# Gated delta scan of a hybrid encoder layer: decaying and adding the state on VectorE instead of GpSimd and VectorE

## The reference

```python
def step(S, xs):
    u0c, wc, qkc, qgc, kdc, glc = xs
    u = u0c - jnp.einsum('bhck,bhkv->bhcv', wc, S)
    o = jnp.einsum('bhck,bhkv->bhcv', qgc, S) + jnp.einsum('bhij,bhjv->bhiv', qkc, u)
    S = glc[..., None, None] * S + jnp.einsum('bhck,bhcv->bhkv', kdc, u)
    return S, o

S, o = lax.scan(step, S0.astype(jnp.float32), (u0, wk, qk, qg, kd, gl))
```

## Time and profile before

| | |
|---|---|
| timed executions, median (lowest to highest) | 2307.71 us (2307.32 to 2307.99) |
| profiled execution, its own time | 2306.37 us |
| its span, first to last instruction | 2305.1 us |
| mean granted TensorE clock, share of full speed | 0.92 |
| `delta_net`, about | 457 to 695 us of the span |
| busy: PE, DVE, ACT, POOL | 2001.3, 1026.7, 686.0, 534.5 us |

### The profile page before, as it was taken

How to read it: one execution, slowest core, us unless ns; L and a number is a source line. 1 busy time by engine, 2 the same in 40 slices (tenths; PEclk the granted TensorE clock), 3 DMA queues, 4 the chain that set the end, 5 groups by cost and what they waited for, 6 DMA issues and landing times. The chain is left out here.

```text
span 2305.1 us, 28427 instructions
## 1 busy us (share of the span) xinstructions
PE 2001.3 (87%) x10881; PEld 1829.8 (79%) x10881; DVE 1026.7 (45%) x1317; ACT 686.0 (30%) x1266; POOL 534.5 (23%) x465
## 2 busy tenths in 40 slices
PE   3999999455883779669999798999999999999997
PEld 3999998254772668559988676899999999999996
DVE  4222443475333321151134122566667575756666
ACT  4112222435552322331131031422222223232322
POOL 2000000232221141430021051223233232332320
PEclk9999999677785779779999899999999999999998
DMA  3222120210003030321013310111010111111012
GB/s 111 59 77 69 56 57 13 72 28 19 28 28 121 1 128 1 127 92 46 10 73 110 126 57 28 46 28 55 27 55 27 55 37 45 48 34 55 27 37 89
DMA packets 122324, 127.00 MB, mean 55 GB/s; under 512 B 10261, under 2 KB 104574, under 8 KB 121950
## 3 DMA queue, kind: packets, MB, share of 16 engines
q1 hardware_dynamic: 117630, 120.89, 16.7%
q10 hardware_dynamic: 3714, 4.76, 0.7%
q0 software_dynamic: 896, 0.19, 0.0%
HBM read 109.86 MB, written 15.96 MB: 55 GB/s over the span
## 5 line engine op out<-in xcount | busy, mean ns | idle before, releaser
L2579 PE MATMUL ffn_banks<-h_hi,up_hi 128*128 128x384 f32 x1056 | 352.9, 334 | 1.8 <-PEq L116 1.8
L2579 PE MATMUL ffn_banks<-h_hi,up_lo 128*128 128x384 f32 x1056 | 353.0, 334 | 0.0
L2579 PE MATMUL ffn_banks<-h_lo,up_hi 128*128 128x384 f32 x1056 | 352.8, 334 | 0.0
L2754 DVE TENSOR_TENSOR h<-h,ffn_banks 128x512 f32<-128x512 f32 x396 | 270.0, 687 | 148.9 <-PE ffn_banks L2614 142.4
L2724 DVE SCALAR_TENSOR_TENSOR ffn_conv_out<-ffn_conv_in,vec,ffn_conv_out 128x1168 f32<-128x1168 f32 x88 | 206.7, 2349 | 128.3 <-ACT ffn_conv_out L2645 122.5
L548 PE MATMUL proj_banks<-x_hi,in_w_hi 128*128 128x384 f32 (+1 forms) x648 | 218.7, 338 | 0.0
L548 PE MATMUL proj_banks<-x_hi,in_w_lo 128*128 128x384 f32 (+1 forms) x648 | 217.3, 335 | 0.0
L548 PE MATMUL proj_banks<-x_lo,in_w_hi 128*128 128x384 f32 (+1 forms) x648 | 217.3, 335 | 0.0
L2579 PEld LDWEIGHTS ffn_banks<-h_hi,up_hi 128*128 128x128 f32 x1056 | 198.2, 188 | 3.0 <-issue 2.0
L2579 PEld LDWEIGHTS ffn_banks<-h_lo,up_hi 128*128 128x128 f32 x1056 | 198.2, 188 | 0.9
L2579 PEld LDWEIGHTS ffn_banks<-h_hi,up_lo 128*128 128x128 f32 x1056 | 198.2, 188 | 0.0
(11 more groups left out here) (409 smaller groups left out, 3612.3 us busy)
## 6 DMA issues: line engine op xcount, KB each, us to landing
up_raw<-in_w_up SPq DMA_DIRECT2D x44, 512.0 KB, 5.8
in_w_raw<-in_w_in SPq DMA_DIRECT2D x22, 512.0 KB, 4.1
down_raw<-in_w_down SPq DMA_DIRECT2D x22, 512.0 KB, 3.6
mem_k_one<-in_cache_mem_k SPq DMA_DIRECT2D x8, 1024.0 KB, 4.9
spill<-mixT SPq DMA_DIRECT2D x10, 576.0 KB, 5.3
wo_w_raw<-in_w_o SPq DMA_DIRECT2D x8, 512.0 KB, 3.7
h<-in_x_prompt SPq DMA_DIRECT2D x8, 512.0 KB, 7.6
mkv_w_raw<-in_w_mk SPq DMA_DIRECT2D x8, 512.0 KB, 3.8
```

The lines of the kernel that those rows point to most:

```text
L2579: ins = nc.tensor.matmul(banks[:, NP * s + p, 0:TC], wt[:, s, k, :], x[:, k, TC * p:TC * p + TC], start=(n == 0), stop=(n == 3 * KD - 1))
L2754: nc.vector.tensor_tensor(to, to, banks[:, d_bank[n % 5], :], ALU.add).then_inc(added, 1)
```

## The change

POOL's `decayed` and its buffer go. VectorE multiplies the old state by the decay and adds the product in one `scalar_tensor_tensor` for each head, in place.

```diff
-        S, Sg, u = (ph.sb(n, [P, HEADS, P]) for n in ("state", "state_decayed", "u"))
+        S, u = (ph.sb(n, [P, HEADS, P]) for n in ("state", "u"))
...
-            def decayed(e, c):
-                n = 2 * (e - 1) + c
-                if n:
-                    pool.wait_ge(s_done, n)
-                end = P * tile_of(e) + 64 * c + 63
-                nc.gpsimd.tensor_tensor(Sg[:], S[:], up[:, :, end:end + 1].to_broadcast([P, HEADS, P]), ALU.mult
-                                        ).then_inc(sg_done, 1)
-
...
             for e in range(1, E_ALL):
-                decayed(e, 0)
                 if e + 1 < E_ALL:
                     q_up(e + 1)
-                decayed(e, 1)
                 if e + 1 < E_ALL:
                     k_tail(e + 1)
                 if e == 1:
...
             def new_state(e, c):
                 n = 2 * (e - 1) + c
                 dve.wait_ge(s_product, n + 1)
-                dve.wait_ge(sg_done, n + 1)
-                nc.vector.tensor_tensor(S[:], Sg[:], banks[2][:], ALU.add).then_inc(s_done, 1)
+                if n:
+                    dve.wait_ge(s_done, n)
+                else:
+                    dve.wait_ge(cleared, 1)
+                    dve.wait_ge(up_done, 3)
+                end = P * tile_of(e) + 64 * c + 63
+                for h in range(HEADS):
+                    ins = nc.vector.scalar_tensor_tensor(S[:, h, :], S[:, h, :], up[:, h, end:end + 1], banks[2][:, h, :],
+                                                         ALU.mult, ALU.add)
+                ins.then_inc(s_done, 1)
```

More of the change, by code:

```diff
@@ L959, in delta_net @@
          l5_wide, rk_done, kd_done, qg_done, z_done, z_copied, x_done, xt_ready, solved, u0_copied, wt_copied,
-         one_ready, one_used, u_s_done, so_done, kds_done, ws_done, u_done, s_product, o_done, sg_done, s_done, o_copied,
+         one_ready, one_used, u_s_done, so_done, kds_done, ws_done, u_done, s_product, o_done, s_done, o_copied,
          squared, rooted, inverted, o_scaled, o_turned, gated, kdm_done, sample_product, sample_decayed,
@@ L966, in delta_net @@
              "z_copied", "x_done", "xt_ready", "solved", "u0_copied", "wt_copied", "one_ready", "one_used", "u_s_done",
-             "so_done", "kds_done", "ws_done", "u_done", "s_product", "o_done", "sg_done", "s_done", "o_copied",
+             "so_done", "kds_done", "ws_done", "u_done", "s_product", "o_done", "s_done", "o_copied",
              "squared", "rooted", "inverted", "o_scaled", "o_turned", "gated", "kdm_done", "sample_product",
```

## The result

The changed kernel took 2319.05 us (median of five, 2314.01 to 2320.37) against 2307.32 us before: ratio 1.0047, 95% interval 1.0033 to 1.0062. The forecast was 2312.8 us, range 2309.0 to 2317.0; the direction was right, the size was not. Timed again beside later experiments, the same kernel gave a ratio of 1.0034 (1.0022 to 1.0047). Its 11 executions average 2317.4 us, and all 108 executions of the kernel before, in all series of measurements, 2307.7. So the loss to be explained is 9.8 us (ahead of rounding), of which 5.1 were forecast. Single executions of one kernel scatter with a standard deviation of 1 to 3 us, in one kernel of 5, so I compare means of groups where I can and give the half-width of their 95% interval where it matters.

What follows compares the result with a forecast made beforehand. VectorE was taken to bound the elimination, TensorE and ScalarE holding each other up the scan. Elimination +4.8 and last tile +0.3 gave +5.1 us on 2307.7: 2312.8 us, range 2309.0 to 2317.0.

Steps and rivals of the forecast that it cites:

- POOL's moved work in the elimination: In delta_net's elimination, four POOL instructions move in and one goes, so it ends 4.8 us later; bounds 0 and 5.7.
- The rival that it is hidden: Moved POOL instructions do not delay VectorE in the elimination; total 2308.0 us, no change; chance 8%.
- not before 545: Sign in the new profile: ScalarE's widening at about 548.1; the forecast is wrong if it still starts before 545.
- The 5.75 us: Upper bound for the elimination's growth, if VectorE gets nothing done during POOL's instructions, as under the exclusive lock.
- Nothing comes back at the scan's start: At the scan's start sample_state(0)'s 2.98 us wait for POOL goes, but this gives no time back.
- Four instructions: In new_state, four take 1.15 us for 0.69, +0.46 a step; only the last tile pays, +0.3, bounds 0 and 0.7.
- the state loop: Rival in the scan: each of 16 steps pays its 0.46 in full, 7.4 us more, total 2320; chance 6%.
- The sum, 4.8 + 0.3: Whole kernel: elimination's 4.8 plus the last tile's 0.3 makes +5.1 us.
- the change should add the same to both: The profiled run and the timed median both grow by 5.1 us: 2306.37 to 2311.5 and 2307.7 to 2312.8.
- The clock rival: Scan meets the granted clock otherwise: 2311.1 or 2309.4, upward 2314.5; downward side 16%, upward counted with the forecast.
- point 3: The part on new_state's four instructions for one: +0.46 a step, +0.3 us on the path in the last tile.

Runs made afterwards that it cites:

- e2: Kernel before, with only POOL's k_tail(2), masked(2), qk_mask(2) and sample_decay(0) moved ahead of decayed(1, 1); 2314.59 us, ratio 1.0027.
- e1: Changed kernel with POOL again waiting for the scan's first new state, so the four POOL instructions leave the elimination; 2314.19 us, ratio 1.0023.
- e9: Changed kernel with the dropped semaphore sg_done still allocated, used by nothing, the buffer still dropped; 2313.76 us.
- e12: Changed kernel measured once more, unaltered, on the chip of e9; 2317.19 us.
- e13: Changed kernel with one other semaphore cleared twice at the stage's end, giving SyncE's list its old length; 2314.52 us.
- e5: Kernel before, with one idle VectorE product of 256 elements ahead of the addition of step 14's state; 2308.97 us, ratio 1.0007.
- e3: Kernel before, with 11 idle VectorE products of 256 elements behind the elimination as a plain delay; 2315.65 us, ratio 1.0031.
- e11: Changed kernel with POOL held ahead of k_tail(0) until the elimination's result is there, and semaphore sg_done kept, used by nothing; 2301.62 us, ratio 0.9970.
- e7: e1 with both the unused buffer state_decayed and the unused semaphore kept at their old places; 2306.97 us, ratio 0.9995.
- e15: e1 measured again, unaltered; 2316.31 us.

## Why the prediction was wrong in its size

1. *POOL's moved work in the elimination, +4.8:* right, 4.7 us (4.65 by VectorE's timeline, 4.76 by ScalarE's wait), and shown alone by e2 (+5.5 for four instructions without one removed) and undone by e1. The rival that it is hidden is out: the widening starts at 547.24, not before 545. The exclusive-lock rule of the Trainium skill ("SBUF — State Buffer", section "SBUF: two separate sides") names the mechanism, and the trace agrees that VectorE's instruction is held for nearly all of POOL's, 2.45 us beside 2.52. The 5.75 us that the prediction worked out by that rule was too high, as the rows had said.
2. *Nothing comes back at the scan's start:* right; sample_state(0) now waits 1.87 us for TensorE.
3. *Four instructions, +0.46 a step, on the path in the last tile alone, +0.3:* right on the instructions (+0.43) and on the place, too small in the price. The wait is 0.40 us, but the eight products behind it run at 1.2 GHz and take 0.9 us more, so that the profile's scan is 1.3 us longer, as it is in the profiles of e9 and e12 (149.5 and 149.6 us; e13's took 151.9). TensorE waits for the state in no middle tile, so the state loop is not the limit. That the wait brings the low clock is supported by e5, where a wait of 0.43 us put there alone is followed by the same slow products; by time e5 puts it at 1.0 to 1.6 us, with an interval that reaches down to none.
4. *The sum, 4.8 + 0.3, and that "the change should add the same to both":* this step failed, in two ways. First, a term was missing. The change drops a semaphore, its diff says so, and I costed the wait and not the clearing. It makes SyncE's list one instruction shorter, which moves a pause onto a load that is waited for: 3.1 us here, 4.5 with POOL quiet. Second, a delay does not cost itself. The idle 5.0 us of e3 cost 7.6 by means (2315.5 against 2307.9 of its chip), e2's 5.5 cost 6.7, and with the list's length restored the changed kernel loses 6.7 for its 5.1. The clock rival had the mechanism and only counted its upward side with the forecast. In e3's profile it is in the scan itself, as the windows of its scan show beside the kernel before's 148.25 us at 0.78:

```profile
548.27:702.13 153.86, 128.01 (x752) 116.02 (x752) 46.59 (x90) 86.25 (x252) 42.94 (x38) 0.75 0.10 28
```

The same 752 matmuls, moved by 5.0 us, took 5.6 us longer at a clock of 0.75 in this execution.

Together: 5.1 as worked out, 3.1 for the list, 1.6 beyond, of 9.8 measured. Of the 1.6, about 1.0 is the last tile's low clock and what else point 3 lacked, by the profile (1.3 for 0.3); the rest was not taken apart. That the rest is the clock is argued from e3 and its profile, and not shown by an experiment of its own; nor is it excluded that the dropped buffer has a share in it, since e9 and e13 lack it too.

The best version is e11: the four instructions, POOL quiet during the elimination, and SyncE's list at its old length, 2301.62 us, ratio 0.9970 (0.9958 to 0.9982), in six executions.

## What to carry to other kernels

When a wait is removed, ask what it kept apart: here a wait on the scan's state kept four POOL instructions with SBUF inputs out of a chain of VectorE instructions with two SBUF inputs, and each went at POOL's pace once they met. Hold such work back on purpose, behind the chain's own semaphore, rather than by luck. And if a small edit moves stages that it does not touch, compare instruction lists by length and position before explaining the time by what the edit computes; an unused semaphore put back is a cheap control. Put back one thing at a time: e7 put back two, and what its buffer does is still open.

## What the runs showed of the hardware that was not expected

SyncE paused for 0.37 to 0.43 us behind the 79th, the 207th and the 335th instruction that it executed, 128 apart, the same in every kernel, so one instruction more or less shifts a pause between a place where SyncE waits anyway and one where a load is due. Behind the 719th, five times 128 further than the 79th, there was none. What the pause is, was not tried; that it is the fetching of instructions is a guess. A single-input VectorE instruction (the normalization, 128x1024, 0.74 us alone) was stretched to 2.73 to 2.85 us beside POOL's split, as the two-input ones were. A wait of 0.40 us on TensorE was followed by eight products at 1.2 GHz, 2.05 us instead of 1.13, so that the two together cost three times the wait. And e9 and the changed kernel, with the same computation in the same order and the same buffers, differ by 3 us on average through one clearing instruction, while executions of one kernel (e15) lie up to 13 us apart.
